# Two transformer blocks on one core: a third output unit begun inside stick-breaking, other banks for head 1, and operations moved in three stages

## The chip, the cores and the metric

The kernel runs on one core of a Trainium2 chip, as one program. The metric is the device time of one execution in microseconds: the median of several runs. The profile is of one more execution. TensorE (PE) multiplies, VectorE (DVE), ScalarE (ACT) and GpSimd (POOL) work on tiles, and SyncE (SP) issues the loads of the weights. Each engine works through its own list in order, and semaphores tie the lists together.

## What is computed

One token block of 512 x 1024 goes through two model blocks: pooling and dilated attention with a gated FFN; then retention with an FFN, and stick-breaking attention with an FFN. The change touches the pooling inside the first mixer, the first FFN's start, and above all stick-breaking:

```python
def stick_breaking(h, w_in, q_gain, k_gain, w_o):
    q, k, v = jnp.split(h @ w_in, 3, axis=-1)            # 16 heads of 64
    q, k, v = rms_norm(heads(q), q_gain), rms_norm(heads(k), k_gain), heads(v)
    z = einsum('bhtd,bhsd->bhts', q, k) * scale           # in blocks of 128 queries
    log_stay = where(mask, log_sigmoid(-z), 0.0)
    later = cumsum(log_stay, reverse=True) - log_stay
    weight = where(mask, exp(log_sigmoid(z) + later), 0.0)
    o = einsum('bhts,bhsd->bhtd', weight, v)
    return o @ w_o

def multi_scale_pool(u, w_pool, pool_scale):              # windows 2, 4, 8, 16
    d = (window_sum(u) / count) - u
    return einsum('bsgc,gcd->bsgd', d, w_pool) * pool_scale
```

## The kernel before, in words

**Weights as units.** All products with weights are cut into units of 128 output rows by 8 (or 11) chunks of 128. A unit is loaded by SP into `RAW[s]` (s is 0 or 1, in turn), cast by ScalarE into its high part `WH[s]` (`split_hi`, L271), and its low part `WL[s] = RAW - WH` is made by GpSimd (`split_lo`, L477). TensorE does three products for each chunk: WH by the input's high part (L290), WH by its low part (L291), and WL by the high part (L299). `high_part` is the first two for all chunks, `low_part` the third. One product of 128 x 512 takes 0.227 us from start to start. GpSimd does nothing else after the start, and a load waits until the pass over its buffer is done.

**Stick-breaking.** Heads go in 8 pairs. Stage j does three units (u for q in bank 0, u+1 for k in bank 1, u+2 for v in bank 0) of pair j, and the attention part of pair a = j - 1. The first stage has no pair a, the next seven have both (one written out, six in a loop of two), and the last has no unit of its own. TensorE's order in a stage with both (`stick_stage`, L913 on) is: unit u, unit u+1, `head_mean(0)`, `high_part(u+2)`, `later(0)`, `low_part(u+2)`, `head_mean(1)`, `later(1)`, `turn_v`, `z` (eight score products into banks 2 to 6), `values`. `later(h)` sums the softplus terms of head h by a triangle of ones (head 0 in banks 2, 3 and a half of 4; head 1 in banks 5, 6 and the other half), from high and low parts SPH and SPL, and XH and XL for added blocks.

VectorE takes the scores (`take_z`, L1830), makes -|z| (`negabs`, L1840), the softplus (L1847), its low part (L1853), added blocks, then the exponent (`exponent`, L1879, three pieces for each head), scales V (L1946) and makes Q and K (`norm_qk`, L1898: QS by a gain by RQ). ScalarE does the exps and logs, the roots (`rn`, L1441 and L1443), the weights' exp (`weights`, L1380) and copies. In the last stage TensorE also works on the first two output units (`some_out`, in banks 0 and 1), chunk by chunk; chunk k needs `M3H` and `M3L` of pair k (`mixed_hi`, `mixed_lo`, L1885). Then `outputs` does the six others in banks 0 and 1 in turn, each after VectorE has added the bank's former content to X (L1507, `s_taken`).

**Attention and pool tiles.** Six pairs of heads go through stages built in the same way (`attn_stage`): scores (L652), `turn_v`, unit, values of the pair before (L683), unit, `turn(0)`, half a unit, `turn(1)` (L668), the other half. Two pool tiles are done on the side, one in stage 0 and one in stage 1 of the attended pair: on VectorE running sums (`pool_sums`, L1575), averages (L1592), differences (L1595), and one product on TensorE (`pool_product`, L631) behind the stage's last unit. The scores of the next stage wait for the copies of the turned probabilities (`copy_probs`, L1663 and L1665).

**FFN 1.** Pairs of units (gate, up) give bank contents that VectorE scales into G (L1487) and U (L1489). The first three units are done together (`first_units_after_post`) and pair 0 uses banks 2 and 3, pair 1 banks 4 and 5, and all later pairs banks 0 and 1; from pair 3 on TensorE waits at bank 0 until the former G is taken.

**Scratch.** Tiles of the different stages lie over each other in SBUF (`scratch`); a third unit's weights RAW3, WH3, WL3 of FFN 1 lie so already.

## Time and profile before

| | us |
|---|---|
| median of 3 runs | 2014.85 |
| lowest and highest | 2013.62, 2014.85 |
| the profiled execution | 2013.68 |
| its span, first to last instruction | 2011.9 |
| TensorE busy | 1983.4 (99%) |
| VectorE, ScalarE, GpSimd busy | 888.5, 767.4, 781.6 (38 to 44%) |
| mean granted TensorE clock | 0.999 |

The span is in us from the first instruction. The attention stages lie between 41 and 184 us, FFN 1 begins at 223, and stick-breaking lies between 1367 and 1622. A timeline row is the start, the duration, the engine, the line, the operation with its tiles, and in brackets the idle time before it with what ended it. Rows with "x8" are several instructions merged.

### The profile page before, as it was taken

The page shows a single profiled execution, that of the slowest core. Times are in us where ns is not written, and L with a number is a line of the kernel's source. Part 1 is how long each engine was busy: PE and PEld are TensorE (multiplying, and loading weights), DVE is VectorE, ACT ScalarE, POOL GpSimd, SP SyncE. Part 2 cuts the span into 40 slices and gives each one's busy share as a digit, 9 for nine tenths or more (in the row PEclk, how much of TensorE's full clock was granted, in tenths as well). Part 3 has the DMA queues.
Part 4 walks back from the last instruction along what each step waited for, and adds up shares of the span by engine and source line. Part 5 has one row for each costly group of instructions (what it writes and reads, how often), then busy time and mean ns, then how long its engine had stood idle before and what let it go on. Part 6 is the DMA issues. An engine that isn't in the chain of part 4 may idle for free.

```text
span 2011.9 us, 25618 instructions
## 1 busy us (share of the span) xinstructions
PE 1983.4 (99%) x8882; PEld 1590.0 (79%) x8882; DVE 888.5 (44%) x1102; ACT 767.4 (38%) x1021; POOL 781.6 (39%) x311
## 2 busy tenths in 40 slices
PE   9999999999999999999999999999999999999999
PEld 6777778888877778787888888887777778888887
DVE  5865643343135334334243343225888854334200
ACT  5664432333233333324332333225666642233211
POOL 3332344444434333243444444443223144444443
PEclk9999999999999999999999999999999999999999
DMA  4112222233323222222232233322111123223322
GB/s 168 63 64 71 77 94 94 94 101 103 101 81 100 68 95 78 70 91 84 86 103 94 95 103 100 101 93 72 60 56 54 40 84 105 94 94 98 109 94 96
DMA packets 48142, 177.31 MB, mean 88 GB/s; under 512 B 5472, under 2 KB 6112, under 8 KB 48096
## 3 DMA queue, kind: packets, MB, share of 16 engines
q1 hardware_dynamic: 46080, 172.55, 25.9%
q10 hardware_dynamic: 2016, 4.13, 0.6%
q8 instruction: 30, 0.49, 0.1%
q14 instruction: 16, 0.13, 0.0%
HBM read 174.57 MB, written 2.10 MB: 88 GB/s over the span
## 4 chain that ended last, share of the span: by engine, by line
PE 85%; DVE 7%; ACT 5%; issue 3%; DMA 0%; DVEq 0%; POOL 0%; ACTq 0%; SPq 0%; POOLq 0%
PE B L290 23%; PE B L291 23%; PE B L299 23%; PE B L824 2%; PE B L814 1%; PE B L818 1%; PE B L815 1%; PE B L931 1%; PE B L310 1%; PE B L311 1%; PE B L312 1%; PE B L865 1%; DVE SPL L1853 1%; PE B L652 1%; ACT SP L1345 1%
## 5 line engine op out<-in xcount | busy, mean ns | idle before, releaser
L477 POOL TENSOR_TENSOR WL<-RAW,WH 128x1024 fp32r<-128x1024 f32 (+1 forms) x302 | 776.6, 2574 | 1214.3 <-PE B L299 770.7
L290 PE MATMUL B<-HH,WH 128*128 128x512 f32 x1608 | 635.4, 395 | 3.4 <-DVE G L1487 2.4
L291 PE MATMUL B<-HL,WH 128*128 128x512 f32 x1608 | 627.0, 390 | 0.0
L271 ACT CAST WH<-RAW 128x1024 fp32r<-128x1024 f32 (+1 forms) x303 | 332.5, 1100 | 569.0 <-PE B L291 503.3
L299 PE MATMUL B<-HH,WL 128*128 128x512 f32 x1608 | 398.8, 390 | 0.0
L290 PEld LDWEIGHTS B<-HH,WH 128*128 128x128 f32 x1608 | 301.9, 188 | 71.8 <-issue 7.9
L291 PEld LDWEIGHTS B<-HL,WH 128*128 128x128 f32 x1608 | 302.2, 188 | 65.1 <-issue 3.4
L299 PEld LDWEIGHTS B<-HH,WL 128*128 128x128 f32 x1608 | 301.1, 188 | 62.3 <-issue 0.5
L291 PE MATMUL B<-ML,WH 128*128 128x512 f32 x462 | 179.9, 389 | 0.0
L290 PE MATMUL B<-MH,WH 128*128 128x512 f32 x462 | 179.9, 389 | 0.0
L1489 DVE TENSOR_TENSOR U<-B,RB 128x512 f32<-128x512 f32 x66 | 45.6, 691 | 296.0 <-PE B L299 296.0
L1492 DVE TENSOR_TENSOR HD<-SG,U 128x512 f32<-128x512 f32 x66 | 148.7, 2253 | 7.4 <-ACT SG L1083 0.7
L1087 ACT CAST MH<-HD 128x512 f32 (+1 forms) x66 | 41.0, 621 | 247.7 <-DVE HD L1492 247.7
L1472 DVE TENSOR_TENSOR ACC<-ACC,SQ 128x512 f32<-128x512 f32 x38 | 80.0, 2105 | 117.2 <-ACT SQ L1062 117.1
L1507 DVE TENSOR_TENSOR X<-X,B 128x512 f32 x32 | 22.0, 687 | 246.8 <-PE B L299 226.2
L299 PE MATMUL B<-MH,WL 128*128 128x512 f32 x462 | 111.6, 389 | 0.0
L299 PEld LDWEIGHTS B<-MH,WL 128*128 128x128 f32 x462 | 86.8, 188 | 18.0
L290 PEld LDWEIGHTS B<-MH,WH 128*128 128x128 f32 x462 | 86.8, 188 | 18.0
L291 PEld LDWEIGHTS B<-ML,WH 128*128 128x128 f32 x462 | 86.8, 188 | 17.9
L1083 ACT ACTIVATE SG<-G 128x512 f32<-128x512 f32 x66 | 41.7, 632 | 88.2 <-DVE G L1487 88.2
L1495 DVE TENSOR_TENSOR ML<-HD,MH 128x512 f32 (+1 forms) x66 | 49.2, 745 | 58.5 <-ACT MH L1087 58.5
L1487 DVE TENSOR_TENSOR G<-B,RB 128x512 f32<-128x512 f32 x66 | 45.6, 692 | 60.4 <-PE B L299 47.0
(269 smaller groups left out, 2180.0 us busy)
## 6 DMA issues: line engine op xcount, KB each, us to landing
RAW<-in_w_small SPq DMA_DIRECT2D x256, 512.0 KB, 3.3
RAW<-in_w_large SPq DMA_DIRECT2D x48, 704.0 KB, 4.0
out_t<-X SPq DMA_DIRECT2D x8, 256.0 KB, 5.6
X<-in_x_t ACTq DMA_DIRECT2D x3, 512.0 KB, 7.1
DECAY<-in_decay ACTq DMA_DIRECT2D x4, 256.0 KB, 2.6
X<-in_x_t ACTq DMA_DIRECT2D x2, 256.0 KB, 4.4
INV<-in_inv_counts SPq DMA_DIRECT2D x1, 512.0 KB, 5.0
BIAS<-in_bias SPq DMA_DIRECT2D x1, 256.0 KB, 3.8
```

The source lines that it names most:

```text
L271: act.copy(WH[u.s][:, 0:chunks, :], RAW[u.s][:, 0:chunks, :]).then_inc(s_hi, units)
L290: pe.matmul(bank, wh[:, c, :], xh[:, k0 + c, :], start=(start and c == 0), stop=False)
L291: mm = pe.matmul(bank, wh[:, c, :], xl[:, k0 + c, :], start=False, stop=False)
L299: mm = pe.matmul(bank, wl[:, c, :], xh[:, k0 + c, :], start=False, stop=(stop and c == chunks - 1))
L477: pool.tensor_tensor(WL[u.s][:, 0:chunks, :], RAW[u.s][:, 0:chunks, :], WH[u.s][:, 0:chunks, :].bitcast(F32), ALU.subtract).then_inc(s_lo, ...
L1083: act.activation(SG[:], G1[:], ACT.Silu).then_inc(s_silu, 1)
L1087: act.copy(MH[:, i, :], HD[:]).then_inc(s_m_hi, 1)
L1472: dve.tensor_tensor(ACC[:], ACC[:], SQ[b][:], ALU.add).then_inc(s_sq_used, 1)
L1487: dve.tensor_tensor(G1[:], gate, RB[:], ALU.mult).then_inc(s_gate, 1)
L1489: dve.tensor_tensor(U1[:], up, RB[:], ALU.mult).then_inc(s_up, 1)
L1492: dve.tensor_tensor(HD[:], SG[:], U1[:], ALU.mult).then_inc(s_hidden, 1)
L1495: dve.tensor_tensor(ML[:, i, :], HD[:], MH[:, i, :].bitcast(F32), ALU.subtract).then_inc(s_m, 1)
```

## The change

It changes the order of work in stick-breaking's stages, begins the output unit U_OUT3+2 (`U_LAST`) in the last of them, and moves pool tile work and banks elsewhere. All products of before are still done.

- In stages with both pairs: TensorE does `head_mean(1)` in front of `low_part(u+2)`. ScalarE casts u+2 in front of `exp_term(1)`, does `rn(1)` right behind `added_hi(1)`, then `weights(0)`, the cast of u+3, `copy_v`, `weights(1)`, the cast of u+4. VectorE does `norm_qk(1)` in front of the whole of `exponent(1)`.
- In the first stage `turn_v` goes behind four of the eight z products.
- In the last stage `U_LAST` is done in bank 5 in pieces of one or two chunks, with weights in RAW4, WH4 (over XH and XL) and WL4 (over QT3). Their load waits for the last use of XH and XL; the cast (`last_hi`) stands in ScalarE's list in front of the last stage, the GpSimd pass behind that of the unit before. Head 1 of this stage sums in banks 2 and 3, each after head 0's exponent piece was taken from it, and VectorE does the first two of these pieces in front of `softplus_lo(1)`. `outputs` starts with the fourth unit.
- FFN 1: pair 2 uses banks 0 and 1, pair 3 banks 2 and 3, and TensorE's wait at pair 3 is for G and U of pair 0.
- Pool tile 0: sums in stage 0, the rest in stage 1; tile 1: sums in stage 2, the rest in stage 3.

```diff
+        _, WL4, _, RAW4, _, WH4, _ = scratch([
+            ("TILES_3", [P, 2 * DC, T]), ("WL4", [P, DC, P], F32R), ("UP_TO_XH", [P, XH_AT]),
+            ("RAW4", [P, DC, P]), ("PAST_RAW4", [P, 2 * P]), ("WH4", [P, DC, P], F32R), ("PAST_WH4", [P, 2 * P])])
+        U_LAST = U_OUT3 + 2
...
-        POOL_DONE = (1, 3)
-        PAIR_DONE = (2, 4, 5, 6, 7, 8)
+        POOL_DONE = (2, 5)
+        PAIR_DONE = (1, 3, 4, 6, 7, 8)
+        POOL_SUMS = {0: 0, 2: 1}
+        POOL_ENDS = {1: 0, 3: 1}
...
+                    sp.wait_ge(b_later, (2 * PAIRS3 - 2) * 3)
+                    sp.wait_ge(s_raw[0], Unit(U_LAST - 2).m * 16 + 16)
+                    sp.dma_start(RAW4[:], stream[at[large] + U_LAST - U_SB]).then_inc(s_raw[0], 16)
+                    load_unit(Unit(U_LAST + 1), stream[at[large] + U_LAST + 1 - U_SB], chunks)
...
+                if first == U_LAST:
+                    pool.wait_ge(s_hi, Unit(U_LAST).index + 1)
+                    pool.wait_ge(b_z, 8 * PAIRS3)
+                    pool.tensor_tensor(WL4[:], RAW4[:], WH4[:].bitcast(F32), ALU.subtract).then_inc(s_lo, 1)
+                    split_lo(Unit(U_LAST + 1), chunks)
...
+                    pe.wait_ge(s_gate, 1)
+                    use_unit(pe, Unit(u0 + 6), B[2][:], DC, HH, HL)
+                    pe.wait_ge(s_up, 1)
+                    use_unit(pe, Unit(u0 + 7), B[3][:], DC, HH, HL)
                 else:
                     pair(0, before)
-                with pe.Fori(3 if before is None else 1, FC) as i:
+                with pe.Fori(4 if before is None else 1, FC) as i:
                     pair(i)
...
+            def some_third(which):
+                if 0 in which:
+                    pe.wait_ge(b_zs, 8 * PAIRS3 - 3)
+                some_chunks(pe, Unit(U_LAST), B[5][:], which, M3H, M3L, ready_m3, weights=(WH4, WL4))
...
                     (b0, b1, (b2, o2)) = LATER_AT[h]
+                    if j is None and h == 1:
+                        b0, b1 = LATER_AT[0][:2]
+                        pe.wait_ge(b_arg, hd * 3 - 2)
...
                 if j is None:
                     some_out(0, range(0, 7))
                     some_out(1, range(0, 4))
+                    some_third(range(0, 2))
                     later(0)
                     some_out(1, range(4, 5))
+                    some_third(range(2, 3))
                     later(1)
                     some_out(1, range(5, 6))
+                    some_third(range(3, 4))
                     values()
                     some_out(1, range(6, 7))
+                    some_third(range(4, 5))
                     finish_out(0)
                     finish_out(1)
+                    some_third(range(5, 7))
+                    finish_unit(pe, Unit(U_LAST), B[5][:], DC, M3H, M3L, ready_m3, weights=(WH4, WL4))
...
                     if a is not None:
                         later(0)
+                        head_mean(1, 1)
                     low_part(pe, u + 2, B[0][:], DC, HH)
                     if a is not None:
-                        head_mean(1, 1)
                         later(1)
                         turn_v()
-                        z()
+                        z(Z_ORDER)
                         values()
                     else:
-                        z()
+                        z(Z_ORDER[:4])
                         turn_v()
+                        z(Z_ORDER[4:])
...
                     log_term(0)
+                if j is not None:
+                    split_hi(act, u + 2, DC)
+                if a is not None:
                     exp_term(1)
                 if j is not None:
-                    split_hi(act, u + 2, DC)
                     squares(0)
...
                     if a is not None:
                         added_hi(1)
-                    split_hi(act, u + 3, DC)
-                    if a is None:
                         rn(1, jj, first)
-                    split_hi(act, u + 4, DC)
-                if a is not None:
-                    weights(0)
-                    if j is not None:
-                        rn(1, jj, first)
-                if a is not None:
-                    weights(1)
-                if j is not None:
-                    copy_v()
+                        weights(0)
+                        split_hi(act, u + 3, DC)
+                        copy_v()
+                        weights(1)
+                        split_hi(act, u + 4, DC)
...
+            def last_hi():
+                act.wait_ge(s_raw[0], Unit(U_LAST).m * 16 + 16)
+                act.wait_ge(b_later, (2 * PAIRS3 - 2) * 3)
+                act.copy(WH4[:], RAW4[:]).then_inc(s_hi, 1)
...
-            ffn(0, U_FFN1, ((2, 3), (4, 5)))
+            ffn(0, U_FFN1, ((2, 3), (4, 5), (0, 1), (2, 3)))
...
                 if a is not None:
+                    if j is None:
+                        exponent(0, range(2))
                     softplus_lo(1)
...
-                if a is not None:
-                    exponent(1, range(1))
                 if j is not None and a is not None:
                     norm_qk(1)
                 if a is not None:
-                    exponent(1, range(1, 3))
+                    exponent(1, range(3))
```

## Rows read from the trace of the kernel before

**Rows 1.** The page's first part: busy time, share of the span, instructions.
```profile
PE 1983.4 (99%) x8882; PEld 1590.0 (79%) x8882; DVE 888.5 (44%) x1102; ACT 767.4 (38%) x1021; POOL 781.6 (39%) x311
```
**Rows 2.** Waits of TensorE, whole span: who waited for whom, total us, times, longest.
```profile
PE B L931 <- DVE KT L1898: 9.7, 7, 1.4
PE B L290 <- DVE G L1487: 2.4, 1, 2.4
...
PE B L942 <- DVE SPL L1853: 1.1, 2, 0.6
PE B L290 <- DVE X L1507: 1.1, 2, 0.8
...
PE B L290 <- ACT VN L1395: 0.7, 1, 0.7
PE B L981 <- ACT LG L1376: 0.5, 1, 0.5
...
PE B L330 <- DVE M3L L1885: 0.5, 1, 0.5
```
**Rows 3.** Timeline of TensorE, one stick-breaking stage with both pairs.
```profile
1434.54 2.06 PE L299 MATMUL B<-HH,WL 128*128 128x512 f32 x8
1436.44 1.02 PE L1000 MATMUL B<-SQ,HEADMEAN 128*128 128x512 f32 x2
...
1441.21 2.52 PE L931 MATMUL B<-QT,KT 64*128 64x512 f32 x16 [1.34 <-DVE KT L1898]
1443.67 2.37 PE L981 MATMUL B<-LG,VN 128*64 128x512 f32 x16
```
**Rows 4.** Timeline of VectorE, the same stage (its z before came at 1411.90).
```profile
1417.13 1.48 DVE L1840 SCALAR_TENSOR_TENSOR SP<-ZS 128x1280 f32<-128x1280 f32 x1
...
1425.30 3.08 DVE L1847 SCALAR_TENSOR_TENSOR SP<-ZS,LG 128x1280 f32<-128x1280 f32 x1 [0.54 <-ACT LG L1353]
...
1436.82 0.69 DVE L1946 TENSOR_TENSOR V<-B,RB 128x512 f32<-128x512 f32 x1
...
1439.49 1.59 DVE L1898 SCALAR_TENSOR_TENSOR KT<-QS,GAINS,RQ 128x512 f32<-128x512 f32 x1 [0.48 <-ACT RQ L1443]
```
**Rows 5.** Timeline of ScalarE, the same stage.
```profile
1434.66 2.00 ACT L271 CAST WH<-RAW 128x1024 fp32r<-128x1024 f32 x2
...
1438.12 0.67 ACT L1441 ACTIVATE RQ<-B,GAINS 128x512 f32<-128x512 f32 x1
```
**Rows 6.** Timeline of GpSimd, the same stage.
```profile
1423.49 3.53 POOL L477 TENSOR_TENSOR WL<-RAW,WH 128x1024 fp32r<-128x1024 f32 x1 [12.20 <-ACT WH L271]
1435.79 4.75 POOL L477 TENSOR_TENSOR WL<-RAW,WH 128x1024 fp32r<-128x1024 f32 x2 [8.76 <-ACT WH L271]
```
**Rows 7.** Waits of TensorE's weight loads in stick-breaking, 1380 to 1660.
```profile
PEld B L942 <- DVE XL L1870: 3.0, 7, 0.4
```
**Rows 8.** Timeline of TensorE, end of stick-breaking.
```profile
1621.15 0.49 PE L290 MATMUL B<-M3H,WH 128*128 128x512 f32 x1 [0.75 <-DVE X L1507]
```
**Rows 9.** Timeline of VectorE, end of stick-breaking (z of the last pair came at 1587.35).
```profile
1591.04 1.49 DVE L1840 SCALAR_TENSOR_TENSOR SP<-ZS 128x1280 f32<-128x1280 f32 x1
...
1615.48 2.14 DVE L1472 TENSOR_TENSOR ACC<-ACC,SQ 128x512 f32<-128x512 f32 x1 [0.95 <-ACT SQ L1062]
```
**Rows 10.** Timeline of GpSimd, end of stick-breaking.
```profile
1614.68 5.20 POOL L477 TENSOR_TENSOR WL<-RAW,WH 128x1024 fp32r<-128x1024 f32 x2 [28.01 <-ACT WH L271]
```
**Rows 11.** Timeline of TensorE, attention: scores of stages 1, 2, 3; a product.
```profile
64.62 2.43 PE L652 MATMUL B<-KT,QT 64*128 64x256 f32 x16
...
89.88 1.13 PE L631 MATMUL B<-DF,WPOOL 128*128 128x512 f32 x2 [0.39 <-DVE DF L1595]
90.93 2.43 PE L652 MATMUL B<-KT,QT 64*128 64x256 f32 x16
...
115.02 2.43 PE L652 MATMUL B<-KT,QT 64*128 64x256 f32 x16
```
**Rows 12.** Timeline of VectorE, attention stage 0: the copies of head 1.
```profile
63.42 0.69 DVE L1663 COPY PT<-B 128x512 f32<-128x512 f32 x1
```

More of the change, by code:

```diff
@@ L312, in start_unit, with some_chunks @@
                 pe.matmul(bank, wl[:, c, :], xh[:, k0 + c, :], start=False, stop=False)
-        def some_chunks(pe, u, bank, which, xh, xl, before):
-            wh, wl = WH[u.s], WL[u.s]
+        def some_chunks(pe, u, bank, which, xh, xl, before, weights=None):
+            wh, wl = weights or (WH[u.s], WL[u.s])
             if 0 in which:
@@ L324, in some_chunks, with finish_unit @@
                 pe.matmul(bank, wl[:, c, :], xh[:, c, :], start=False, stop=False)
-        def finish_unit(pe, u, bank, chunks, xh, xl, before, k0=0, stop=True):
-            wh, wl, c = WH[u.s], WL[u.s], chunks - 1
+        def finish_unit(pe, u, bank, chunks, xh, xl, before, k0=0, stop=True, weights=None):
+            (wh, wl), c = weights or (WH[u.s], WL[u.s]), chunks - 1
             before(k0 + c)
@@ L457, in _ @@
                     start = U_THIRD // 2 + 1
+                if first == U_SB:
+                    with sp.Fori(start, (U_LAST - U_SB) // 2) as i:
+                        for n in range(2):
+                            load_unit(Unit(first + n, i, 2), stream[i * 2 + (at[large] + n)], chunks)
+                    sp.wait_ge(b_later, (2 * PAIRS3 - 2) * 3)
+                    sp.wait_ge(s_raw[0], Unit(U_LAST - 2).m * 16 + 16)
+                    sp.dma_start(RAW4[:], stream[at[large] + U_LAST - U_SB]).then_inc(s_raw[0], 16)
+                    load_unit(Unit(U_LAST + 1), stream[at[large] + U_LAST + 1 - U_SB], chunks)
+                    start = (U_LAST - U_SB) // 2 + 1
                 with sp.Fori(start, count // 2) as i:
@@ L589, in outputs @@
                     two(0, before)
-                with pe.Fori(1, DC // 2) as i:
+                if started > 2:
+                    two(1, skip=1)
+                with pe.Fori(2 if started > 2 else 1, DC // 2) as i:
                     two(i)
@@ L762, in _ @@
             attn_stage(None, PAIRS1 - 1)
-            outputs(0, U_OUT1, 1, DC, M1H, M1L, ready_m1, started=True)
+            outputs(0, U_OUT1, 1, DC, M1H, M1L, ready_m1, started=2)
             mean_of_post(1)
@@ L917, in stick_stage, with z @@
                 first_a = isinstance(a, int) and a == 0
-                def z():
+                def z(order):
                     pe.wait_ge(b_qk, jj * 2 + 2)
-                    for h, sb_, bank, at in ((0, 0, 2, 0), (1, 0, 5, 0), (0, 2, 4, 0), (1, 1, 6, 0), (0, 1, 3, 0),
-                                             (1, 2, 4, 256), (0, 3, 3, 384), (1, 3, 6, 384)):
+                    for h, sb_, bank, at in order:
                         w = t_width(sb_)
@@ L1044, in _ @@
             stick_stage(None, None, PAIRS3 - 1, 1)
-            outputs(4, U_OUT3, 1, DC, M3H, M3L, ready_m3, started=True)
+            outputs(4, U_OUT3, 1, DC, M3H, M3L, ready_m3, started=3)
             pe.wait_ge(s_taken, 8 * 5 - 1)
@@ L1222, in attn_stage @@
                         mixed_hi(a)
-                if a in (0, 1) and j is not None:
-                    pool_scale(a)
+                if a in POOL_ENDS and j is not None:
+                    pool_scale(POOL_ENDS[a])
             attn_stage(0, None)
@@ L1499, in ffn, with outputs, two @@
                     pair(i, B[0][:], B[1][:])
-            def outputs(o, n, u0, per, post, which=None, g=None, by_halves=False):
-                def two(i):
+            def outputs(o, n, u0, per, post, which=None, g=None, by_halves=False, third=None):
+                def two(i, banks=(0, 1)):
                     for b in range(2):
@@ L1506, in two @@
                             wait_unit(dve, Unit(u0 + (2 + b if by_halves else per * b + per - 1), i, 2 * per))
-                            dve.tensor_tensor(X[:, c, :], X[:, c, :], B[b][:], ALU.add).then_inc(s_taken, 1)
+                            dve.tensor_tensor(X[:, c, :], X[:, c, :], B[banks[b]][:], ALU.add).then_inc(s_taken, 1)
                         if n is not None:
@@ L1514, in outputs @@
                     zero_sum(n)
-                with dve.Fori(0, DC // 2 - (1 if post else 0)) as i:
+                if third is not None:
+                    two(0)
+                    two(1, (third, 1))
+                with dve.Fori(0 if third is None else 2, DC // 2 - (1 if post else 0)) as i:
                     two(i)
@@ L1676, in attn_stage @@
                     rotate(0)
-                    if a in (1, 2):
-                        pool_lo(a - 1)
+                    if a is not None and a - 1 in POOL_ENDS:
+                        pool_lo(POOL_ENDS[a - 1])
                 if a is not None and not first_a:
@@ L1877, in exponent @@
                         bank, o, at, w = LATER_PIECES[h][n]
+                        if j is None and n < 2:
+                            bank = LATER_PIECES[0][n][0]
                         dve.wait_ge(b_later, hd * 3 + n + 1)
@@ L1938, in stick_stage @@
                 if a is not None:
-                    exponent(0, range(3))
+                    exponent(0, range(3) if j is not None else range(2, 3))
                 if j is not None and a is None:
@@ L1962, in _ @@
             stick_stage(None, None, PAIRS3 - 1, 1)
-            outputs(4, 7, U_OUT3, 1, False, 5, G_FFN3)
+            outputs(4, 7, U_OUT3, 1, False, 5, G_FFN3, third=5)
             rnorm(7)
```

51 lines of the change are left out of this document (31 added, 20 removed).

## The prediction

> **What bounds the kernel now.** I read the page's first part, then the waits of TensorE, then a timeline of one stage on every engine. TensorE is busy 99% of the span [rows 1], and the granted clock is 0.999 (2.4 GHz), so no edit can win more than TensorE's idle time, 28.5 us, and some restarts behind it. The list of TensorE's waits says where the idle time is [rows 2]: 9.7 us in 7 waits for KT in stick-breaking, 2.4 us in one wait at FFN 1, 3.2 us at the end of stick-breaking (SPL 1.1, X 1.1, LG 0.5, M3L 0.5), 0.7 us for VN in the first stick-breaking stage. Each term below is one of these rows; the question is always what is late next.
>
> **The seven stages of stick-breaking that have both a new pair and an old one.** TensorE ends the turning of V and then waits 1.34 us for `norm_qk(1)`, which makes KT [rows 3, 4]. Three causes lie behind that. The mean of head 1's squares is issued behind `low_part` (1436.44), so its root on ScalarE starts at 1438.12, behind two weight casts (2.00) and `weights(0)` [rows 3, 5]. KT sits on VectorE behind `exponent(1, range(1))`. And its row lasts 1.59 us where QT's form needs some 0.7: it starts at 1439.49 while GpSimd's pair of weight passes runs from 1435.79 to 1440.54 [rows 4, 6]. The same shows at 1425.30: a softplus of 1.48 us lasted 3.08 because GpSimd ran until 1427.02, and 1427.02 plus about 1.4 is its end [rows 4, 6].
>
> The change moves the mean ahead of `low_part`, the root ahead of `weights(0)` and of both casts, and KT ahead of `exponent(1)`. Counted from the start of `later(0)` (0): the mean's matmul ends at about 3.2, the root is there at 4.6, `low_part` (1.90, [rows 3]) ends at 5.05, V is scaled by 5.75 and KT by 6.4. The second sum and the turning of V end at 7.6. KT is then 1.2 us early, and GpSimd's first pass starts at 6.85, behind it. So the wait goes whole: 9.7 us, and some 0.07 us of each restart, 10.2 us. What is late next? `exponent(1)` ends at 8.0 and its last bank is wanted at 8.5; no wait. ScalarE now runs cast u+3 (5.8 to 6.8), `copy_v` (from 7.7, it waits for the turning), `weights(1)` (8.2 to 9.5), cast u+4 (to 10.4); `values` wants `weights(1)` at 7.6 + 2.46 [rows 3] = 10.1. That leaves 0.5 us, the smallest margin of the change. The casts release GpSimd's passes and the load behind each (3.3 us to landing): the load for the next u+2 is issued when the pass of u+3 ends, 1.7 us after the score products (z) start, and wanted 9.4 after, so both queues stay hidden.
>
> The other move in these stages, cast u+2 ahead of `exp_term(1)`, lets GpSimd's pass start when unit u ends (10.75 after z started, not 11.6 as at 1423.49 [rows 6]); it then blocks the first softplus instead of the second, and the VectorE chain comes out about 0.5 us earlier. `later(0)` waits now for XL, up to 0.4 us on the weight queue in 7 waits [rows 7]; of that 0.1 us each is on the path: 0.7 us. Bounds for this part: 9.7 and 11.2; taken 10.9.
>
> **The first stage.** The turning of V goes between the z products, so the 0.7 us wait for VN [rows 2] is covered by the last four of them. But VectorE takes the first z's only when all eight are done, which the turning delays by 0.6 us, and the chain behind reaches `later(0)` no earlier than before. I count 0.1 us (bounds 0 and 0.7).
>
> **The end of stick-breaking.** The third output unit (24 matmuls, some 5.4 us) is no new work; it moves into the gaps. If every gap is filled, 3.2 us and six restarts of 0.1 us go: 3.75 us. Against that stands the order on GpSimd. Cast u+4 now ends about 2.8 us after z starts (it came before z), so the pass of that unit runs from 2.9 to 5.3, and the pass of the new WL4 is queued behind it. VectorE's `negabs(0)` is asked for 3.69 us after z (1591.04 against 1587.35) and reads SBUF twice [rows 9]. It waits until 5.3, which is 1.6 late; WL4 then runs to 9.15, and `negabs(1)`, ready at 8.35, waits 0.8 more. That VectorE gets its turn between two passes is shown at 1615.48: an add lasted 2.14 while two passes ran as 5.20 from 1614.68 [rows 9, 10]. `mixed_lo` of pair 6 is queued behind `negabs(1)` and is 2.4 late, so TensorE stands before chunk 6 of the first output for 2.35 us, where it hardly stood. Everything behind moves with it; the second sum costs 0.3 more, since two exponent pieces now stand before `softplus_lo(1)`. Gain 3.75 - 2.65 = 1.1 us. Unit U_OUT3+3 then waits for X of columns 0 and 1 as now (1621.15, [rows 8]), some 0.8 us behind the third unit. Bounds -0.5 and 3.75; I take 1.1 because the rows of a blocked operation are this close in form.
>
> The Trainium skill, page "SBUF — State Buffer", section "SBUF: two separate sides", says that a Vector operation with two SBUF inputs and a GpSimd operation that reads SBUF hold the shared port pair one at a time, for the whole instruction. The four rows above agree; by a shared-bandwidth reading instead, the end would give nearer 3 us.
>
> **FFN 1.** Pairs 0 to 3 get banks (2,3), (4,5), (0,1), (2,3). TensorE's wait of 2.4 us for G [rows 2] was for bank 0 of a fourth pair; banks 2 and 3 were read long before, and the next time TensorE needs bank 0 the pair's G is 3 us old. The cast of unit 7 is there 1.6 us before its use. 2.4 + 0.1 = 2.5 us (bounds 2.0 and 2.6).
>
> **Pool tiles in attention.** A stage with a pool tile and values lasts 90.93 - 64.62 = 26.31, one without 115.02 - 90.93 = 24.09, and the product itself 90.93 - 89.88 = 1.05 [rows 11]; so 1.17 us are waits. The change leaves the sums in stages 0 and 2 and moves averages, differences and product to stages 1 and 3. Stage 0 loses the product, but its scores wait for VectorE's copies, which start at 63.42 behind the differences [rows 12] and would start at 62.8: scores at 63.9 for 64.62, 0.7 won. Stage 1 becomes 24.09 + 1.05: 1.2 won. Stage 2 gets the four sums: `turn(1)` 0.66 late, and the copies end 0.8 behind `low_part` with no product to cover them: 1.5 lost. Stage 3 gets the product: 1.05 lost. Net 0.6 us lost (bounds: 1.0 won, 1.5 lost).
>
> **The sum.** 10.9 + 0.1 + 1.1 + 2.5 - 0.6 = 14.0 us. The profiled execution took 2013.68 (span 2011.9), so its like would take 1999.7; the median of the three runs is 2014.85, which gives 2000.9. I forecast 2000.3.
>
> **The rivals.**
> A, the end is not blocked: the passes find their time, the full 3.75 us come: 14.0 + 2.7, 1997.6. For it: a delay of 0.9 us on ScalarE could put WL4 behind `negabs(1)`. Against: rows 9 and 10.
> B, the wait changes its name: `values` waits for `weights(1)`. Margin 0.5 us; with ScalarE 1.2 us later than I count, 0.7 us in seven stages, 4.9: 2005.2. For it: ScalarE gets a wait for the turning in front of `weights(1)` with a cast ahead of it.
> C, the KT wait stays, because V, which waits for `low_part`, is in front of KT and `low_part` is 0.9 us later. Then the loop gives 0.7 and the sum is 3.8: 2010.5. Against: KT has 1.2 us in the count above.
> D, slower: GpSimd's passes of u+3 and u+4 leave the place behind the casts (1435.79 to 1440.54) and come 6.85 to 9.25 and 10.4 to 12.8 after `later(0)`, the second into the two-input operations of the next chain (`negabs(0)` at 1417.13, 5.2 after z [rows 4]). I count 0.1 us of conflict there. A chain delay d above the 0.4 us that it has to spare lengthens each of seven stages by d - 0.4; all gain is gone at 7 (d - 0.4) = 14.0, d = 2.4, one whole pass. If both passes block in full, d = 4.8, and the time is 2014.3 + 30.8 - 14.0 = 2031. Against: unit u's end holds the softplus anyway, which hides 1.9 us of it. The page named above gives this rule its ground.
>
> **How the numbers follow.** Forecast 0.64, A 0.13, B 0.13, C 0.06, D 0.04. About 0.2% (4 us) is what a measurement of this kernel can tell from no change. Faster by more than that: the forecast, A, B and a little of C, 0.90; within: 0.05; slower: 0.05. The bounds of the terms add to 7.5 (9.7 less 2 for a small stall at `values`, 0, -0.5, 2.0, -1.5) and to 19 us, so 1995.3 to 2006.8; this takes in A and B and leaves out C and D. Range 1995.5 to 2006.5.
>
> **What would show it.** Right: no wait for KT; stages of 27.8 us between z rows where they are 29.3; KT rows of 0.75 us; the FFN 1 wait gone; a wait of over 2 us for M3L inside the first output of the end, and `negabs` rows of some 3 us; attention stage 2 at 25.6 us. Wrong: a wait for LG at `values` (B), for KT (C) or for SPL or XL at `later(0)` (D); an end of stick-breaking without the M3L wait (A); a wait for a landing of RAW4 or for s_lo at the third unit, which I hold to be 5 us early.

## The result, and the profile after

The changed kernel takes 1999.66 us in the median of 4 runs (1998.35 to 2000.49), the kernel before beside it 2014.85 (2013.62 to 2014.91): a ratio of 0.9925, 95% interval 0.9908 to 0.9943. The forecast was 2000.3. The profiled execution took 2000.36 with a span of 1998.6 us, 13.3 less than the span before.

The page's first part and the waits of TensorE, whole span, answer to [rows 1, 2] (engine and line waited for whom, total us, times, longest):

```profile
PE 1982.1 (99%) x8882; PEld 1591.5 (80%) x8882; DVE 884.1 (44%) x1102; ACT 768.4 (38%) x1021; POOL 776.4 (39%) x311
```
```profile
PE B L333 <- DVE M3L L1957: 1.8, 1, 1.8
PE B L689 <- DVE PT L1735: 1.5, 2, 0.7
...
PE B L705 <- DVE PT L1735: 1.1, 3, 0.5
PE B L301 <- DVE X L1574: 1.1, 2, 0.8
...
PE B L984 <- DVE XL L1940: 0.6, 1, 0.6
...
PE B L984 <- DVE SPL L1923: 0.3, 1, 0.3
```

The seven waits for KT, the wait for G in FFN 1, and those for VN and LG are gone. New at the top stands one wait for M3L; in attention, waits for PT have taken the place of those for DF; and the first stick-breaking stage now waits 0.59 us for XL.

**One stage with both pairs** (TensorE and VectorE, timeline; they answer to [rows 3, 4]):

```profile
1428.91 0.33 PE L984 MATMUL B<-XH,ALL 128*128 128x384 f32 x1
...
1430.36 1.07 PE L1048 MATMUL B<-SQ,HEADMEAN 128*128 128x512 f32 x2
...
1435.03 0.62 PE L1037 MATMUL B<-IDENT,V 128*128 128x128 f32 x4
1435.58 2.53 PE L973 MATMUL B<-QT,KT 64*128 64x512 f32 x16
```
```profile
1419.40 4.48 DVE L1917 SCALAR_TENSOR_TENSOR SP<-ZS,LG 128x1280 f32<-128x1280 f32 x2
...
1433.32 0.69 DVE L2020 TENSOR_TENSOR V<-B,RB 128x512 f32<-128x512 f32 x1 [0.80 <-PE B L310]
1433.93 0.75 DVE L1970 SCALAR_TENSOR_TENSOR KT<-QS,GAINS,RQ 128x512 f32<-128x512 f32 x1
```

The score products (z) follow the turning of V at once, and KT is done 0.9 us ahead of them, in a row of 0.75 us where it was 1.59. From z to z the stage lasts 27.46 us (1408.12, 1435.58, and five more up to 1572.84), where it lasted 29.25. The two softplus, of which GpSimd now blocks one, come as one row of 4.48: 1.48 and 3.0.

**The end** (VectorE, then GpSimd, then TensorE; they answer to [rows 8 to 10]; the last z came at 1572.84):

```profile
1576.53 2.96 DVE L1910 SCALAR_TENSOR_TENSOR SP<-ZS 128x1280 f32<-128x1280 f32 x1
...
1581.12 2.00 DVE L1910 SCALAR_TENSOR_TENSOR SP<-ZS 128x1280 f32<-128x1280 f32 x1
1583.04 0.68 DVE L1957 TENSOR_TENSOR M3L<-B,M3H 128x512 fp32r<-128x512 f32 x1
```
```profile
1575.77 2.37 POOL L501 TENSOR_TENSOR WL<-RAW,WH 128x1024 fp32r<-128x1024 f32 x1 [1.06 <-ACT WH L282]
1578.11 3.66 POOL L531 TENSOR_TENSOR WL<-RAW,WH 128x1024 fp32r<-128x1024 f32 x1
```
```profile
1583.77 0.50 PE L333 MATMUL B<-M3H,WH 128*128 128x512 f32 x1 [1.77 <-DVE M3L L1957]
1584.11 0.39 PE L334 MATMUL B<-M3L,WH 128*128 128x512 f32 x1
...
1584.95 0.63 PE L334 MATMUL B<-M3L,WH 128*128 128x512 f32 x1
...
1607.27 0.50 PE L301 MATMUL B<-M3H,WH 128*128 128x512 f32 x1 [0.80 <-DVE X L1574]
...
1613.28 0.49 PE L301 MATMUL B<-M3H,WH 128*128 128x512 f32 x1 [0.26 <-DVE X L1574]
```

`negabs(0)` needs 1.48 us and lasts 2.96: it ends at 1579.49, 1.35 us behind the end of GpSimd's first pass (1578.14), nearly its whole own length, so it began when the pass ended. The pass of WL4 (L531) then lasts 3.66 instead of 2.37, because it waits in its turn for `negabs(0)`; and `negabs(1)` ends 1.35 us behind that one. M3L is late, and TensorE waits 1.77 us. Behind the wait stands what no step of the prediction had: the products start 0.43 us apart instead of 0.23. The windows say why (each line: stretch; PE, weight loads, VectorE, ScalarE, GpSimd busy; granted clock; DMA share, GB/s):

```profile
1584.00:1586.00 2.00, 2.00 (x7) 1.59 (x7) 1.12 (x1) 1.27 (x2) 0.00 (x0) 0.65 0.29 115
1586.00:1588.00 2.00, 2.00 (x7) 1.54 (x6) 1.56 (x2) 1.58 (x2) 0.00 (x0) 0.50 0.00 0
1588.00:1590.00 2.00, 2.00 (x10) 1.67 (x9) 1.34 (x1) 0.63 (x1) 0.00 (x0) 0.99 0.00 0
```

The granted clock fell to 0.50, the lower of its two levels (1.2 GHz), and came back at 1588.2. From the last z to unit U_OUT3+3 it takes 34.43 us where it took 33.80.

**Attention** (TensorE; it answers to [rows 11]; stage 0's scores start at 40.63 here, at 40.95 before):

```profile
63.59 2.43 PE L689 MATMUL B<-KT,QT 64*128 64x256 f32 x16 [0.74 <-DVE PT L1735]
...
88.58 2.43 PE L689 MATMUL B<-KT,QT 64*128 64x256 f32 x16
...
114.19 2.43 PE L689 MATMUL B<-KT,QT 64*128 64x256 f32 x16 [0.73 <-DVE PT L1735]
...
139.14 2.43 PE L689 MATMUL B<-KT,QT 64*128 64x256 f32 x16
```

Four stages of 22.96, 24.99, 25.61 and 24.95 us make 98.51, where they made 98.20.

### The profile page after: what moved, and what is told of

It reads as the page before. It is cut to its first block, busy times and chain, and to the rows that moved or that the text cites. A ratio compares the mean times of both kernels' runs of the same rounds, so it can differ in the third digit from the quotient of the medians.

```text
span 1998.6 us, 25555 instructions
## 1 busy us (share of the span) xinstructions
PE 1982.1 (99%) x8882; PEld 1591.5 (80%) x8882; DVE 884.1 (44%) x1102; ACT 768.4 (38%) x1021; POOL 776.4 (39%) x311
## 4 chain that ended last, share of the span: by engine, by line
PE 93%; DVE 3%; ACT 2%; issue 1%; DMA 0%; POOL 0%; DVEq 0%; SPq 0%; ACTq 0%; POOLq 0%
PE B L301 25%; PE B L302 25%; PE B L310 25%; PE B L861 2%; PE B L984 2%; PE B L851 1%; PE B L855 1%; PE B L852 1%; PE B L973 1%; PE B L321 1%; PE B L323 1%; PE B L322 1%; PE B L902 1%; PE B L1029 1%; PE B L689 1%
## 5 line engine op out<-in xcount | busy, mean ns | idle before, releaser
L501 POOL TENSOR_TENSOR WL<-RAW,WH 128x1024 fp32r<-128x1024 f32 (+1 forms) x301 | 767.7, 2552 | 1206.3 <-PE B L310 792.8
L1574 DVE TENSOR_TENSOR X<-X,B 128x512 f32 (+1 forms) x32 | 22.0, 687 | 244.9 <-PE B L310 224.0
```

The costliest lines, as they stand in the source:

```text
L501: pool.tensor_tensor(WL[u.s][:, 0:chunks, :], RAW[u.s][:, 0:chunks, :], WH[u.s][:, 0:chunks, :].bitcast(F32), ALU.subtract).then_inc(s_lo, ...
```

## The experiments

Spans of single profiles differ by a fall of the clock here and there (below), so I compare pieces between the starts of two rows of TensorE: A, attention, from the first to the fifth of its six scores rows; F, from there to the first z; L, first z to last z; E, last z to the row of low products (weights' low part) of unit U_OUT3+4. Where the expectations say "the first to the last scores row", they mean A. Before: A 98.20, F 1244.64, L 203.56, E 43.01. After: A 98.51, F 1242.10, L 191.60, E 44.19. Each edit is made on the changed kernel. A time from a single run has no interval; there the pieces carry the reading.

### The changed kernel once more

> The changed kernel, unaltered, beside the others on their chip. Its first profile had the granted clock at 0.98 in the first 100 us (a start 1.3 us later than in two later profiles of other kernels with 1.00 there) and at 0.50 to 0.65 from 1584 to 1588 us, right behind the product that waited 1.77 us for M3L. My theory: the fall behind that wait comes in most executions and costs about 1.6 us each time, so a profile with 1.00 throughout and the same wait would lie near 1998.4 and the others between 1999 and 2000.5. Rival: the fall there has nothing to do with the wait, and comes and goes as that of the first 100 us does; then it shows in some of the kernels without the wait as well.

Measured: 1998.82 us (1997.60 to 2000.43, 5 runs; before beside it 2014.65; ratio 0.9924, 0.9910 to 0.9937). The profiled execution has the same wait for M3L, and no fall (TensorE's row, then the window behind it; the next reads 1.00 too):

```profile
1582.61 0.50 PE L333 MATMUL B<-M3H,WH 128*128 128x512 f32 x1 [1.77 <-DVE M3L L1957]
```
```profile
1584.00:1586.00 2.00, 2.00 (x11) 1.65 (x10) 0.72 (x1) 2.00 (x2) 0.00 (x0) 1.00 0.00 0
```

From the last z to U_OUT3+3 it takes 32.82 us here (1571.68 to 1604.50), against 34.43: a fall costs 1.61. Whether it comes "in most executions" these runs don't tell: one profile of the two has it, and a mean clock of 0.999 can be this fall or another. This profile also has a granted clock of 1.00 in the first 20 us, where before and after had 0.91, and its first scores row comes at 39.54 instead of 40.63: 1.1 us more. The two together, 2.7 us, are about what lies between the fastest and the slowest run of this kernel here (2.8).

### M3L between the two passes

```diff
                     if j is None:
                         negabs(0)
+                        mixed_lo(a - 1)
                     take_z(1)
                     if j is None:
                         negabs(1)
-                        mixed_lo(a - 1)
```

> The changed kernel with one move in VectorE's list of the last stick-breaking stage: mixed_lo of pair 6 right behind negabs(0), in front of take_z(1). In the changed kernel TensorE stands 1.77 us before chunk 6 of the first output, because M3L of pair 6 is queued behind negabs(1), and its clock then falls to the lower level (two products of 128x512 that start 0.23 us apart before start 0.43 apart behind it, 8 of them). Theory: the queue position alone makes the wait, and the wait makes the clock fall. Then the wait goes, the clock stays at 1.00 through 1575 to 1600, later(0) starts about 14.7 us after the last z instead of 17.4, and unit U_OUT3+3 starts 31.7 instead of 34.4 us after it: profiled time 2.7 us shorter, 1997.6. negabs(1) no longer waits for GpSimd (row 1.5 instead of 2.0), since it is asked for 0.6 us later. Rival: the clock falls because of what TensorE did in z and values (turned and half-width products), whatever the wait: then only about 1.1 us come, and the slow products are seen again.

Measured: 1996.95 us (1996.03 to 1997.67, 4 runs), ratio 0.9921 (0.9904 to 0.9938) to a before of 2013.04 on that chip. E is 41.52, 2.67 less than after; to U_OUT3+3 it is 31.76. The granted clock is 1.00 in all four runs. VectorE, then GpSimd:

```profile
1575.25 2.96 DVE L1910 SCALAR_TENSOR_TENSOR SP<-ZS 128x1280 f32<-128x1280 f32 x1
1578.13 0.68 DVE L1957 TENSOR_TENSOR M3L<-B,M3H 128x512 fp32r<-128x512 f32 x1
...
1580.44 1.49 DVE L1910 SCALAR_TENSOR_TENSOR SP<-ZS 128x1280 f32<-128x1280 f32 x1
```
```profile
1576.83 3.67 POOL L531 TENSOR_TENSOR WL<-RAW,WH 128x1024 fp32r<-128x1024 f32 x1
```

`negabs(0)` is as blocked as it was, but M3L, which reads one bank and one SBUF tile, no longer stands behind `negabs(1)`; it takes its plain 0.68 us inside GpSimd's row, and the wait is gone from the list. Of the 2.67 us, 1.61 are the fall and 1.06 the wait: the rest of the wait comes back as a wait of 0.73 for SPL. The theory holds for the wait; for the fall it is only in keeping with it, since the changed kernel with its wait ran without a fall too.

### Both z's taken ahead of the first negabs

```diff
                     take_z(0)
+                    take_z(1)
                     if j is None:
                         negabs(0)
-                    take_z(1)
-                    if j is None:
+                        mixed_lo(a - 1)
                         negabs(1)
-                        mixed_lo(a - 1)
```

> The changed kernel with VectorE's last stage in the order of the loop: take_z(0), take_z(1), negabs(0), mixed_lo, negabs(1). Theory of the exclusive pair, where the operation that asks first runs whole: negabs(0) is asked for at about 5.3 us after z, when GpSimd's pass of unit U_OUT3+1 ends and WL4's pass has been waiting in its queue; WL4 gets it, the negabs(0) row lasts 3.8 us instead of 2.96 and ends at 9.1 instead of 6.6 after z. The chain of head 0 is 2.5 us later than in e1_lo_early, and unit U_OUT3+3 starts about 34.2 us after z (31.7 there). Rival, where VectorE wins at the boundary between two GpSimd passes whoever asked first: negabs(0) lasts 1.5, ends at 6.8, and the end is as in e1_lo_early.

Measured: 1997.89 us in one run; to U_OUT3+3 it is 31.68 us, E 41.46, as with M3L early; no wait for M3L. VectorE and GpSimd:

```profile
1578.24 1.50 DVE L1910 SCALAR_TENSOR_TENSOR SP<-ZS 128x1280 f32<-128x1280 f32 x1
1579.66 0.68 DVE L1957 TENSOR_TENSOR M3L<-B,M3H 128x512 fp32r<-128x512 f32 x1
1580.26 3.10 DVE L1910 SCALAR_TENSOR_TENSOR SP<-ZS 128x1280 f32<-128x1280 f32 x1
```
```profile
1576.01 2.39 POOL L501 TENSOR_TENSOR WL<-RAW,WH 128x1024 fp32r<-128x1024 f32 x1 [1.05 <-ACT WH L282]
1578.34 3.67 POOL L531 TENSOR_TENSOR WL<-RAW,WH 128x1024 fp32r<-128x1024 f32 x1
```

The times are the rival's. `negabs(0)` reached VectorE's head as the first pass ended, took the gap in 1.50 us, and GpSimd's second pass waited for it (3.67). But its row starts at 1578.24 and that of the second pass at 1578.34, so the run doesn't show that VectorE wins whoever asked first: it may itself have been first. `negabs(1)` then lasted 3.10, but nothing on the path stood close behind it. So VectorE's chain loses 1.99 us as changed (1.48 and 0.51), 1.48 with M3L early and some 1.6 here, always less than a pass of 2.37; what costs TensorE time is what is queued behind the loss.

### No third output

```diff
-                    some_third(range(0, 2))
...
-                    some_third(range(5, 7))
-                    finish_unit(pe, Unit(U_LAST), B[5][:], DC, M3H, M3L, ready_m3, weights=(WH4, WL4))
...
-            outputs(4, U_OUT3, 1, DC, M3H, M3L, ready_m3, started=3)
+            outputs(4, U_OUT3, 1, DC, M3H, M3L, ready_m3, started=2)
```

(the edit also takes out the other pieces of `some_third`, and what SP, ScalarE, GpSimd and VectorE do for this unit)

> The changed kernel without the third output unit in the last stage (U_LAST is done in bank 0 by outputs, as before); head 1 still sums in banks 2 and 3, and all other parts of the change stay. Theory: GpSimd's pass of unit U_OUT3+1 alone blocks negabs(0) (row 2.9), WL4's is gone so negabs(1) lasts 1.5; the chain is 1.6 us later than in the kernel before, and unit U_OUT3+3 starts about 35.4 us after the last z (33.8 before, 34.4 with the third unit). So the third unit is worth 1.0 us as the change has it and 2.6 once its wait and slow clock are gone; time 2001.3. Rival: the third unit is what makes the end slower (its pass, its order), and without it the end takes 33.8 or less; time at or below 1999.7.

Measured: 2000.60 us in one run; 35.66 us to U_OUT3+3, and E 44.87. The theory had 35.4, the rival at most 33.8: the third unit makes the end shorter. TensorE waits 1.28 for M3L, 0.52 and 0.98 for SPL, 0.54 for LG, 0.52 for M3L again, 0.32 and 0.76 for X. The first of them:

```profile
1582.82 0.50 PE L333 MATMUL B<-M3H,WH 128*128 128x512 f32 x1 [1.28 <-DVE M3L L1944]
```

Without WL4's pass `negabs(1)` lasts 1.49 instead of 2.00 and the wait for M3L is 0.49 shorter: that is the price of this pass, where I had counted 0.8. And the third output with all that comes with it is worth 44.87 - (44.19 - 1.61) = 2.3 us.

### exp_term(1) ahead of the cast again

```diff
-                if j is not None:
-                    split_hi(act, u + 2, DC)
                 if a is not None:
                     exp_term(1)
                 if j is not None:
+                    split_hi(act, u + 2, DC)
                     squares(0)
```

> The changed kernel with ScalarE's cast of u+2 behind exp_term(1) again, as before the change. I had counted 0.1 us a stage for what the early cast brings; the stages came out 0.25 shorter than my sum. Theory: the early cast gives GpSimd its pass before the first softplus instead of between the two, so XL is ready when later(0) wants it: without it later(0) takes 2.2 us instead of 1.9 (SPL's product to XH's 0.41 us apart instead of 0.23), stages last 27.75 instead of 27.46, 2.0 us in seven; time 2001.6 to 2002.4. Rival: the 0.25 us came from the other moves, and the stages stay at 27.46.

Measured: 2001.50 us in one run. The stages last 27.74 us (1407.46 to 1573.92 for six), 0.29 more than after. TensorE:

```profile
1428.42 0.44 PE L984 MATMUL B<-XH,ALL 128*128 128x384 f32 x1
1428.71 0.34 PE L984 MATMUL B<-XL,ALL 128*128 128x384 f32 x1
```

The row of XH lasts 0.44 and XL comes 0.29 behind it, as before the change; after it, XH's row lasts 0.33 and XL starts 0.17 behind. XH's row itself starts 0.40 behind that of SPL (1428.02), where it is 0.23 after. The first sum stands for XL again. So the cast's move ahead, which lets GpSimd's pass block the first softplus instead of the second, is worth 0.29 us in a stage, all of it in this one wait. L is 193.97, 2.4 more than after: 1.74 of it in six stages, and 0.63 in the first, where the wait for XL is 1.21 us instead of 0.59. The theory holds, and the cast is worth more than I had.

### The mean behind the low part again

```diff
                         later(0)
-                        head_mean(1, 1)
                     low_part(pe, u + 2, B[0][:], DC, HH)
                     if a is not None:
+                        head_mean(1, 1)
                         later(1)
```

> In the stages with both pairs the mean of head 1's squares is put back behind the low part of unit u+2; the root, the weights, the casts and KT keep their new places. Counted from the start of the sum later(0), with the changed kernel's rows: the mean ends at 4.7 instead of 2.9, the root is there at 5.8, KT by 6.6 where the score products come at 7.1. So TensorE still doesn't wait for KT. But the root stands ahead of weights(0), the cast, the copy of V and weights(1) on ScalarE: these end near 10.1, where the value products want them at 9.6. Theory: rival B of the prediction comes true, a wait of 0.5 to 0.7 us for LG in seven stages, stages of 28.0 to 28.1 instead of 27.46 between score rows, the whole 4 to 4.5 us longer. Rival: the place of the mean is what removed the wait for KT, and with it put back TensorE waits for KT again, by 0.5 us or more in each of the seven.

Measured: 2002.52 us (2002.13 and 2002.90), ratio 0.9943 (0.9923 to 0.9963). The stages last 28.03 us as forecast, but for a reason that neither side had. ScalarE, VectorE, TensorE:

```profile
1432.76 0.69 ACT L1507 ACTIVATE RQ<-B,GAINS 128x512 f32<-128x512 f32 x1 [2.80 <-PE B L1048]
```
```profile
1434.15 0.75 DVE L1970 SCALAR_TENSOR_TENSOR KT<-QS,GAINS,RQ 128x512 f32<-128x512 f32 x1 [1.45 <-ACT RQ L1509]
```
```profile
1435.56 2.60 PE L973 MATMUL B<-QT,KT 64*128 64x512 f32 x16 [0.42 <-DVE LG L1951]
1438.08 2.37 PE L1029 MATMUL B<-LG,VN 128*64 128x512 f32 x16
```

KT is in time (ready at 1434.90), and `weights(1)` too (its row ends at 1437.87, the values start at 1438.08). It is VectorE's turn that is lost: it stands 1.45 us for RQ with KT at its head, the whole of `exponent(1)` is queued behind, and the next z needs the banks that it empties. With the mean early that stand is gone. The place of the mean is worth 0.57 of the 1.79 us, although the wait for KT goes without it. The earlier root and the earlier KT, which are left as what removes that wait, were not put back one by one.

### The pool tiles' order of before

```diff
-        POOL_DONE = (2, 5)
-        PAIR_DONE = (1, 3, 4, 6, 7, 8)
+        POOL_DONE = (1, 3)
+        PAIR_DONE = (2, 4, 5, 6, 7, 8)
-        POOL_SUMS = {0: 0, 2: 1}
-        POOL_ENDS = {1: 0, 3: 1}
+        POOL_SUMS = {0: 0, 1: 1}
+        POOL_ENDS = {0: 0, 1: 1}
```

(and TensorE's wait in `pool_product` as before)

> Only the order of the sums and of the averages in the attention put back as it was before the change. The prediction charged the new order with 0.6 us, of which the profiles show 0.3 (98.51 against 98.20 from the first to the last scores row). Theory: the stretch goes back to 98.2, with waits of 0.39 and 0.50 for PT and two of 0.39 for DF, and everything behind it is unchanged. Rival: the order before was tied to the rest of the kernel before, and in this kernel it costs a wait more: 98.5 or longer.

Measured: A 98.16 us, with the waits for PT (0.39, 0.50) and DF (0.39, 0.37) back; 1999.42 us (1998.54 and 2000.31). The theory holds in A: this part of the change costs 0.35 us there, which the times of whole runs are too scattered to show.

### The sums behind the copy of the weights

```diff
                 if j is not None:
-                    if a in POOL_SUMS:
-                        pool_sums(POOL_SUMS[a])
                     times_cos(1)
                 if a is not None:
                     copy_probs(0)
                 if j is not None:
                     if first:
                         take_pools()
+                    if a in POOL_SUMS:
+                        pool_sums(POOL_SUMS[a])
```

(and tile 1's third and fourth sum go to the start of `pool_averages`)

> Only the averaging sums moved behind the copy of the softmax weights, with tile 1's four sums split between two stages. Theory: the three waits for PT that are left in stages 0 and 2 (0.39 and 0.74, 0.51 and 0.73) are VectorE's queue behind the sums, of which one beside a GpSimd pass lasts 2.77 instead of 0.69; moved, they go, and the attention stretch from the first to the last scores row falls from 98.5 to 95.9 to 96.2, the whole by 2.3 to 2.6. Rival: the sums fall beside the next GpSimd pass or in front of the second copy, and only the first waits go (0.9): 97.6.

Measured: 1996.13 us (1995.70 and 1996.56), ratio 0.9908 (0.9890 to 0.9926), 2.7 us less than the changed kernel beside it (1998.82); A is 95.63, a little below the 95.9 to 96.2 expected. TensorE has no wait of note left between 36 and 145. VectorE in stage 0:

```profile
56.04 0.68 DVE L1733 COPY PT<-B 128x512 f32<-128x512 f32 x1
...
56.97 1.45 DVE L1645 TENSOR_TENSOR WA<-UP 128x512 f32<-128x512 f32 x1
```

The copies come ahead of the sums, of which one lasts 1.45 beside GpSimd; in the changed kernel one lasted 2.77 and stood ahead of the copies. That makes 2.9 us, for waits of 2.4: as at the end, where a wait of 0.26 made a unit's step 0.54 longer, a wait costs more than the idle time in its row, since a product that need not wait starts before the end of the one ahead of it.

### The three together

```diff
                         negabs(0)
+                        mixed_lo(a - 1)
...
                         negabs(1)
-                        mixed_lo(a - 1)
...
+                    for b in range(ahead):
+                        c = i * 2 + b
+                        wait_unit(dve, Unit(u0 + b, i, 2))
+                        dve.tensor_tensor(X[:, c, :], X[:, c, :], B[banks[b]][:], ALU.add).then_inc(s_taken, 1)
...
-                    two(0)
+                    two(0, ahead=2)
```

(with the sums behind the copy)

> Three edits on the changed kernel: M3L between the two blocked passes (measured alone: the stretch from the last z row to the third unit's end 2.7 shorter), the averaging sums behind the copy of the weights and tile 1's four sums spread over two stages (2.4 to 2.6 expected), and in the output's pairs the first addition of both X chunks ahead (the waits of 0.80 and 0.26 for X gone, 1.0). Sum 6.1 to 6.3 off the changed kernel beside it, so 1993.5 where that stands at 1999.7. Rival: what is taken from VectorE's queue at one place comes back as a wait of the next unit (X's second halves, or the averages for the pooled product); then 1 to 2 us of the 6.2 are missing, and each has a new wait row on X or DF.

Measured: 1994.63 us (1994.11 to 1995.16, 4 runs), ratio 0.9901 (0.9886 to 0.9917), where the changed kernel beside it stands at 1998.82: 4.2 us less, not 6.2. A is 95.63 and E 41.54, that of M3L early alone. The X edit gives nothing. TensorE and VectorE:

```profile
1600.56 0.47 PE L301 MATMUL B<-M3H,WH 128*128 128x512 f32 x1 [0.37 <-ACT WH L282]
...
1607.00 0.49 PE L301 MATMUL B<-M3H,WH 128*128 128x512 f32 x1 [0.73 <-DVE X L1578]
```
```profile
1603.38 2.88 DVE L1544 SCALAR_TENSOR_TENSOR HL<-X,GAINS,HH 128x512 fp32r<-128x512 f32 x1
1606.17 0.68 DVE L1578 TENSOR_TENSOR X<-X,B 128x512 f32<-128x512 f32 x1
```

U_OUT3+3 starts 0.43 us earlier, and then U_OUT3+4 waits 0.73 for an X that stands behind an HL lasting 2.88 us: the rival of that expectation. Of the 2.0 us that are missing this is 1.0. The rest is no wait that came back (A gave 0.4 more than counted, E for M3L what it gave alone): the expectation had the fall at its full price of 1.6 in its 2.7, and not every execution of the changed kernel pays it. How many do was not counted, so this last part is argued.

### The wait for M3L made longer

```diff
                     if j is None:
                         negabs(1)
-                        mixed_lo(a - 1)
...
                     softplus(0)
                     if j is None:
+                        mixed_lo(a - 1)
                         softplus_lo(0)
```

> Only the wait for M3L at the end of stick-breaking is lengthened: VectorE makes M3L behind the first softplus, 1.45 us later. The five profiles with a wait of 1.77 to 1.79 us there had the clock at 0.50 behind it in three and at 1.00 in two, the four profiles without it or with 1.28 had 1.00. The wait should become 3.2 us, and the stretch from the last z row to the start of the fourth unit 32.8 + 1.45 = 34.3 us where the clock stays, 35.9 where it falls. Theory: the length of the wait decides, so now the clock falls in every execution: all four runs show a mean clock of at most 0.999, and the median is 1.45 + some 0.8 (the part that half the executions of the changed kernel escape) = 2.2 us above it. Rival: the fall comes by chance about every second time, whatever the length: 1.45 more, and a run or two with a clock of 1.00.

Measured: 2000.10 us (1999.64 to 2001.94, 4 runs); mean granted clocks 0.998, 1.000, 0.999 and 0.999. The profile has the longer wait and the fall (a window of 0.50 from 1586 to 1588), with 35.68 us to U_OUT3+3:

```profile
1585.49 0.80 PE L333 MATMUL B<-M3H,WH 128*128 128x512 f32 x1 [3.20 <-DVE M3L L1957]
```

But one run of four shows a clock of 1.000, where every profile with a fall has 0.999 or less, and the median is 1.3 us above the changed kernel's 1998.82 (that of another chip), about the 1.45 of the wait and no more. So the theory is out: a longer wait did not make the fall certain. That it comes by chance every second time, as the rival has it, four runs don't show.

### FFN 1 put back

```diff
-                    pe.wait_ge(s_gate, 1)
-                    use_unit(pe, Unit(u0 + 6), B[2][:], DC, HH, HL)
-                    pe.wait_ge(s_up, 1)
-                    use_unit(pe, Unit(u0 + 7), B[3][:], DC, HH, HL)
...
-            ffn(0, U_FFN1, ((2, 3), (4, 5), (0, 1), (2, 3)))
+            ffn(0, U_FFN1, ((2, 3), (4, 5)))
```

> Only FFN 1 put back: pair 2 in banks 0 and 1 is followed by a pair 3 in the same banks, behind the wait for the G of pair 2. Theory: the wait of 2.4 us for G is back, and the first stick-breaking score row comes 2.4 to 2.5 us later, counted from the attention's last scores row; nothing else changes: some 2001.3 for a profile without a fall of the clock at the end, 2003 with one. Rival: part of the 2.4 us had come back elsewhere in FFN 1 of the changed kernel (a wait for HL, WL or G further on), then less than 2.2 are lost.

Measured: 2002.04 us in one run. F is 1246.28, 4.18 us longer than after, and 1.64 longer than in the kernel before, which has the same wait. TensorE, and the windows:

```profile
261.37 0.79 PE L301 MATMUL B<-HH,WH 128*128 128x512 f32 x1 [2.39 <-DVE G L1549]
261.96 0.63 PE L302 MATMUL B<-HL,WH 128*128 128x512 f32 x1
```
```profile
260.00:262.00 2.00, 0.63 (x2) 0.54 (x3) 1.90 (x4) 0.74 (x2) 0.08 (x1) 0.84 0.37 90
262.00:264.00 2.00, 2.00 (x6) 1.61 (x5) 1.11 (x2) 1.35 (x2) 1.09 (x1) 0.50 0.42 172
```

A fall again, behind a wait that had none in the profile of before. Without it (the first eight products take 3.51 us, 1.94 before) 2.6 us remain, as forecast for the wait.

## Why the prediction was right, and where it was not

**The seven stages: mechanism right, one term mis-sized.** The wait for KT went whole; the mean's place was not needed for that, so it went by the order of root and KT, of which neither was tried alone. The margins held (KT 0.9 us early, counted 1.2; `values` with no wait). Six stages gained 1.79 us each where 1.56 were counted. The step that failed is the wait for XL: I put 0.1 of its 0.4 us on the path. `later(0)` lasts 1.91 us (1428.45 to 1430.36) where it lasted 2.22, so 0.31 were, and the cast put back brings 0.29 of them back. The seven gave 11.96 us where 11.0 were counted with the first stage.

**The first stage.** It gained 1.23 where the seven-stage count gave it 1.56 and 0.1 more: VectorE takes the z's later, as I wrote, and now TensorE waits 0.59 us for XL in the first sum (1.21 where the cast is put back). The loss was named and counted 0.4 too low.

**The end: right to U_OUT3+3, and then two things missing.** `negabs(0)` was blocked for 1.48 us (counted 1.6), `negabs(1)` for 0.5 (0.8), and M3L came as the wait that was forecast, 1.77 us (2.35). The Trainium skill, page "SBUF — State Buffer", section "SBUF: two separate sides", has the exclusive hold in both directions, and here GpSimd's rows of 3.66 and 3.67 show the other direction. Where the clock stays up the piece lasts 32.82 us, so 0.98 are gained where 1.1 were counted. Not counted was that unit U_OUT3+4 then waits for X too: from one unit's low products to the next's it takes 5.98 us instead of 5.44, 0.54 lost. And not counted was the clock: a new wait was priced at its length, while in four of the eight profiles that have this wait at 1.77 us or longer it cost 1.4 to 1.6 us more.

**FFN 1.** 2.54 us (2.5 counted).

**Attention.** Stages of 22.96, 24.99, 25.61 and 24.95 against 22.95, 25.14, 25.6 and 25.14: 0.31 lost (0.6). The count was right in its parts, but it took the waits for PT as given: the sums ahead of the copy cost 2.9 us in this order, eight to nine times what the order itself costs.

**The sum.** Three small slips in the prediction's adding don't touch the forecast: 3.2 us and six restarts of 0.1 are 3.8 and not 3.75, the lower bounds add to 7.7 and not 7.5, and the upper to 19.25. In the two profiles: 14.0 counted; 0.96 more from the loop, 0.3 from attention and 0.3 from a start that both kernels share; 0.12 less to U_OUT3+3, 0.54 for its neighbour's X, 1.61 for the fall: 13.3, as measured. That the forecast lay 0.6 us from the median is in part luck: these errors are set against each other. The medians differ by 15.2, more than the profiles, probably since the changed kernel's profile had a fall at the end and that of before had none at FFN 1, where its wait can have one as well (it had one with FFN 1 put back).

**The rivals.** A (not blocked) is out by the rows of the end, D by the stages. B's wait came in none of the seven stages; with the mean put back a wait for LG did come, but for the arguments in the banks, not for the weights. C would have needed KT late even with the mean in front, and even with the mean behind it was not.

## What to carry to other kernels

When two GpSimd passes came to lie beside this VectorE chain, the chain lost 1.5 to 2.0 us in each of three orders of its operations; so ask what is queued behind those with two SBUF inputs, and take what TensorE waits for (here M3L, which reads PSUM) out of that queue. Price a new wait of TensorE not only at its length: here one of 1.8 us cost 1.6 us more in three of six profiles, and where it was taken away (M3L between the two passes) all four runs have a mean clock of 1.00. And an operation at the head of its engine's queue that stands for its input can cost through what is behind it, even when it is itself in time: the early mean paid 0.57 us a stage through `exponent(1)`, not through KT.

## What was not expected of the hardware

The granted clock fell from 1.00 to 0.50 in mid-kernel for some 3.4 us at single waits of TensorE, in kernels that were busy ahead of them. Of ten waits of 1.77 to 3.20 us in the profiles, five had a fall, which began between 0.3 us ahead of the wait's end (the 3.20) and 1.5 us behind it: of 1.77 (changed kernel; pool order of before), 1.78 (`exp_term(1)` first), 2.39 (FFN 1 put back) and 3.20; five had none: 1.77 (changed kernel again), 1.79 twice (sums late; FFN 1 put back, at the end), 2.10 (mean behind) and 2.39 (kernel before). Outside the first 20 us none was seen behind a wait of 1.45 us or less, of which the kernel before has seven of 1.3 to 1.5. One kernel with the same wait has it in one execution and not in the next. The other fall is that of the first 20 us, with a granted clock of 0.91 there in six of the thirteen profiles, of the kernel before too. There it came at some 11 us and behind short waits: those six, and none of the others, have a wait of TensorE of 0.38 to 1.04 us between 7.2 and 8.2 us, ahead of two of up to 0.75 and 0.41 us at 9 and 10 us that all thirteen have. Whether that wait brings the fall was not tried. What decides between fall and no fall in mid-kernel stays open: the length of the wait does not by itself. A kernel that fills the wait with other products was not tried.
